# Expert outputs scaled as they are stored and summed into the residual during the last expert, expert biases added at the start, and two norms computed as one chain

## The reference, cut to what matters

```python
def moe(h, ...):                       # h: (512, 1024)
    logits = h @ w_router + b_router   # 32 experts
    top_vals, top_idx = top_k(logits, 4); weights = softmax(top_vals)
    # for every token and each of its four experts e:
    gu = x @ w_gu[e] + b_gu[e]; gate, up = split(gu)
    act = (clip(up, -7, 7) + 1) * min(gate, 7) * sigmoid(1.702 * min(gate, 7))
    y += weight * (act @ w_down[e] + b_down[e])

h = h + g2 * moe(modulate(rmsnorm(h, norm_mlp_w), sh2, sc2), ...)
x = rmsnorm(h, final_norm_w)           # end of the first block
p = rms_norm(x, even_norm) @ even_w_in # start of the second block; x is also its residual
```

## Time and profile before

| | us |
|---|---|
| median of three runs (2360.0 to 2361.71) | 2360.09 |
| the profiled execution, its own time | 2359.39 |
| its span, first to last instruction | 2357.4 |
| TensorE busy | 2215.9 (94%) |
| VectorE busy | 738.2 (31%) |
| mean granted TensorE clock | 0.973 |

### The profile page before, as it was taken

One profiled execution on the slowest core, in us unless ns is written; L12 is line 12 of the kernel. 1 busy time (PEld: TensorE's weight loads), 2 busy tenths in 40 slices (PEclk: granted clock), 3 DMA queues, 4 the chain that ended last, 5 costly groups with the idle time before them and its releaser, 6 DMA issues. The chain is left out here.

```text
span 2357.4 us, 35769 instructions
## 1 busy us (share of the span) xinstructions
PE 2215.9 (94%) x14443; PEld 907.7 (39%) x14443; DVE 738.2 (31%) x1371; ACT 501.8 (21%) x912; POOL 141.1 (6%) x174
## 2 busy tenths in 40 slices
PE   5999877999999999999999972999999998999998
PEld 2434532333333333333333321455445444444443
DVE  1133447222121222222222216003077004356533
ACT  2121222111110111111111102110126002446530
POOL 0000002110011111011111012000000000000000
PEclk9999988999999999999999985999999999999999
DMA  9138529999999999999999943412220121122200
GB/s 362 54 122 312 196 103 356 407 411 416 417 417 415 414 415 417 416 414 417 414 416 414 411 164 120 165 54 101 72 71 1 61 82 39 60 90 90 71 36 36
DMA packets 143111, 556.63 MB, mean 236 GB/s; under 512 B 18485, under 2 KB 34014, under 8 KB 109170
## 3 DMA queue, kind: packets, MB, share of 16 engines
q1 hardware_dynamic: 118662, 512.67, 55.1%
q0 software_dynamic: 10608, 30.31, 3.5%
q10 hardware_dynamic: 13788, 12.93, 1.6%
HBM read 535.78 MB, written 25.03 MB: 238 GB/s over the span
## 5 line engine op out<-in xcount | busy, mean ns | idle before, releaser
L1822 PE MATMUL ps<-ring,xeT 128*32 128x512 f32 x6144 | 669.4, 595 | 6.2 <-ACT xeT L1533 6.2
L1822 PEld LDWEIGHTS ps<-ring,xeT 128*32 128x32 f32 x6144 | 196.3, 110 | 451.1 <-issue 449.0
L1799 PE MATMUL ps<-ring,aT 128*32 128x512 f32 x2048 | 266.4, 592 | 1.0 <-ACT ysb L1637 1.0
L1693 DVE TENSOR_SCALAR gate<-ps 128x768 f32<-128x768 f32 x32 | 30.7, 958 | 551.8 <-PE ps L1822 551.8
L1625 ACT ACTIVATE sig<-gate 128x768 f32<-128x768 f32 x32 | 27.0, 844 | 701.1 <-DVE gate L1693 701.1
L360 PE MATMUL ps<-hT_late,ring 128*128 128x512 f32 x384 | 165.2, 592 | 1.5 <-PEq L2046 1.5
L1807 PE MATMUL ps<-ring,aT 128*32 128x256 f32 x2048 | 157.1, 379 | 0.0
L1807 PEld LDWEIGHTS ps<-ring,aT 128*32 128x32 f32 x2048 | 66.0, 110 | 153.7 <-issue 153.7
L2733 PE MATMUL ps<-hT_late,ring 128*128 128x512 f32 x256 | 110.6, 592 | 1.6 <-PEq L2492 1.6
L360 PE MATMUL ps<-ring,mT 128*128 128x512 f32 x256 | 110.1, 592 | 1.2 <-PEq L2299 1.2
L2746 PE MATMUL ps<-hT_late,ring 128*128 128x512 f32 x256 | 110.5, 592 | 0.0
(11 more groups left out here) (374 smaller groups left out, 2030.7 us busy)
## 6 DMA issues: line engine op xcount, KB each, us to landing
ring<-in_w_gu SPq DMA_DIRECT2D x256, 1024.0 KB, 8.3
ring<-in_w_down SPq DMA_DIRECT2D x128, 1024.0 KB, 7.6
ring<-in_even_w_in SPq DMA_DIRECT2D x18, 1024.0 KB, 6.5
ring<-in_w_ada SPq DMA_DIRECT2D x32, 512.0 KB, 8.3
ring<-in_odd_w_in SPq DMA_DIRECT2D x32, 512.0 KB, 5.2
ring<-in_w_ada SPq DMA_DIRECT2D x8, 1024.0 KB, 23.4
ring<-in_w_in SPq DMA_DIRECT2D x8, 1024.0 KB, 14.5
y_scratch<-ysb ACTq DMA_DIRECT2D x128, 64.0 KB
```

The costliest lines, as they stand in the source:

```text
L1693: nc.vector.tensor_scalar(thirds(gate[:]), part_banks(0), 7.0, None, ALU.min).then_inc(M.gu_read, 1)
L1799: mm = nc.tensor.matmul(quad(Y0, 2 * q + n), acted(k, q), w[:, kk, n * BANK:(n + 1) * BANK], start=first, stop=last)
L1822: mm = nc.tensor.matmul(quad(q, c), left(q), part_columns(w, c), start=start, stop=stop)
```

## The change: what it does

- **Scaling at the store.** ScalarE no longer copies rows from PSUM. VectorE does it in one product with `g2q` (g2 laid out as the rows are) at the end of each step (`read_y`). `g2q` is made by eight copies at the very start of the experts' part.
- **Biases.** b_down times g2, by the turned weights, is four products for each half of the columns: the first half after step 0, the second in the middle of step 1. VectorE adds them to `res` (`add_bias`, four of 128x512 each).
- **Sums during the last expert.** Steps 0, 1 and 31 are written out, steps 2 to 30 are the loop. GpSimd gathers the 16 rows of tiles of experts 0 to 29 as soon as these are stored (weights are zero where the row belongs to a later expert), then four of expert 30, then four of expert 31. VectorE adds each straight to `res` (`sum_rows`), 8 ahead of its work for step 31, 4 behind it, 4 after expert 30's rows are read, and 4 after expert 31's are.
- **The end of the experts.** `down(32)` writes other banks and reads a separate transposed tile (`last_turned`), and there is no product for row numbers ahead of it. The last stores are issued by ScalarE and SyncE, four each.
- **One chain for two norms.** With h = `res` and hw = h * w1b, both sums of squares are taken at once; the second norm's scale is worked out from the two (`pair`). xn = hw * scale is handed to TensorE; the four tiles of `res` are written after that.
- **Places.** hT_late and mT are allocated ahead of the experts and lend their room to the experts' buffers; sgT serves for two buffers of later layers. Seven even-layer weight tiles are loaded in the combining part.

```diff
+                for h in range(2):
+                    for q in range(2):
+                        part = slice((2 * q + h) * QUAD, (2 * q + h + 1) * QUAD)
+                        listing.on(nc.vector.tensor_copy(
+                            g2q[part, 0:2], g2b[part, h * BANK:(h + 1) * BANK].rearrange("p (b n) -> p b n", b=2)))
+                for c in range(4):
+                    part = slice(c * QUAD, (c + 1) * QUAD)
+                    listing.on(nc.vector.tensor_copy(g2q[part, 2], g2b[part, c * 256:(c + 1) * 256]))
                 split_places(list_step, posm[:], place[:], third_of[:])
...
                     nc.vector.transpose(turned[:, 0:W], up[:, 0:W]).then_inc(M.aT_read, 1)
+                    if not first:
+                        read_y(e, Y0)
+
+                def read_y(e, b):
+
+                    dve.wait_ge(M.y_stored, e * 128)
+                    nc.vector.tensor_tensor(thirds(ysb), ps[:, b:b + 2, :].rearrange("p b (h n) -> p (b h) n", h=2)[:, 0:3], g2q,
+                                            ALU.mult).then_inc(M.y_read, 1)
+
+                def add_bias(h):
+
+                    for t in range(NT):
+                        dve.wait_ge(biased.sem, NT * h + t + 1)
+                        cols = slice(h * BANK, (h + 1) * BANK)
+                        bias_added.on(nc.vector.tensor_tensor(res[:, t, cols], res[:, t, cols], bank(Y0 + t), ALU.add))
...
                 weights_and_rows()
+                prepare(0)
+                bdown_loaded.wait(dve)
+                bias_ready.on(nc.vector.tensor_tensor(bdown, bdown, g2b[:], ALU.mult))
+                dve.wait_ge(M.aT_done, 1)
+                bias_ready.on(nc.vector.tensor_copy(wT[:], ps[:, IDS, P:2 * P]))
                 block_step(0, True)
+                add_bias(0)
...
+                prepare(1)
+                add_bias(1)
+                block_step(1, False)
...
+                with dve.Fori(0, E - 3) as i:
+                    prepare(i + 2)
+                    block_step(i + 2, False)
...
+                sum_rows(0, 2 * TOPK)
+                block_step(E - 1, False, last=True)
+                sum_rows(2 * TOPK, 3 * TOPK)
+                dve.wait_ge(M.y_done, 2 * (E - 1))
+                read_y(E - 1, Y0)
+                sum_rows(3 * TOPK, NT * TOPK)
+                dve.wait_ge(M.y_done, 2 * E)
+                read_y(E, Y0 + 2)
+                sum_rows(NT * TOPK, NT * TOPK + NT)
...
+                pool.wait_ge(M.y_stored, 128 * (BEFORE + 1))
+                for n in range(NT * TOPK + NT):
+                    if n >= GB:
+                        pool.wait_ge(row_used.sem, n - GB + 1)
+                    if n == NT * TOPK:
+                        pool.wait_ge(M.y_stored, 128 * (BEFORE + 2))
...
+                pool.wait_ge(M.y_stored, 128 * (E + 1))
+                for t in range(NT):
+                    last_rowed[t].on(nc.gpsimd.indirect_dma_start(
...
-                down(E, 8 + 12 * (E - 1), 0, final=True)
+                block_step(E - 1, 8 + 12 * (E - 2), 0, False, last=True)
+                down(E, 8 + 12 * (E - 1), 0, Y0 + 2, last_turned)
...
+                def join(t):
+                    last_rowed[t].wait(dve)
+                    h_ready.on(nc.vector.scalar_tensor_tensor(out=res[:, t, :], in0=last_rows[:, t, :], scalar=w_end[:, 1, t:t + 1],
+                                                              in1=res[:, t, :], op0=ALU.mult, op1=ALU.add))
+                    h_ready.wait(dve)
+                    h_ready.on(nc.vector.tensor_tensor(hw[:, t, :], res[:, t, :], w1b[:], ALU.mult))
...
+                w1b_loaded.wait(dve)
+                join(0)
+                join(1)
+                means(0)
+                join(2)
+                scale(0)
+                means(1)
+                join(3)
+                scale(1)
+                means(2)
+                scale(2)
+                means(3)
+                scale(3)
                 for t in range(NT):
+                    nc.vector.tensor_scalar(res[:, t, :], hw[:, t, :], pair[:, t, 2:3], None, ALU.mult)
```

More of the change, by code:

```diff
@@ L1619, in _, with block_step @@
                 parted.on(nc.scalar.copy(bparts[third], bgu[third]))
-                def block_step(e, first):
+                def block_step(e, first, last=False):
                     act.wait_ge(M.gu_read, e * 2 + 1)
@@ L1704, in block_step @@
                     dve.wait_ge(M.act_ready, e + 1)
+                    if last:
+                        nc.vector.transpose(last_turned[:, 0:W], up[:, 0:W]).then_inc(M.aT_read, 1)
+                        return
                     if not first:
@@ new lines, in _, with sum_rows @@
+                step(nc.vector.memset(gbuf, 0.0))
+                parted.wait(dve)
+                step(nc.vector.memset(last_rows, 0.0))
+                step(nc.vector.memset(turned[:, W:], 0.0))
+                list_ready.on(nc.vector.memset(rowstat[:, 7, 0:1], 0.0))
+                with dve.Fori(0, E - 3) as i:
+                    prepare(i + 2)
+                    block_step(i + 2, False)
+                def sum_rows(n0, n1):
+                    bias_added.wait(dve)
+                    for n in range(n0, n1):
+                        t = n // TOPK if n < NT * TOPK else n - NT * TOPK
+                        w = w_early[:, n:n + 1] if n < NT * TOPK else w_end[:, 0, t:t + 1]
+                        dve.wait_ge(rowed[n % GB].sem, 16 * (n // GB + 1))
+                        if n:
+                            row_used.wait(dve)
+                        row_used.on(nc.vector.scalar_tensor_tensor(out=res[:, t, :], in0=gbuf[:, n % GB, :], scalar=w,
+                                                                   in1=res[:, t, :], op0=ALU.mult, op1=ALU.add))
@@ L1812, in down, with acted, add_biases @@
                             mm.then_inc(stream.used, 1)
-                def acted(k, q):
+                def acted(k, q, src):
                     at = q * FQ + k * QUAD
-                    return turned[:, at:at + QUAD]
+                    return (turned if src is None else src)[:, at:at + QUAD]
+                def add_biases(h):
+                    for t in range(NT):
+                        rows = slice(t * E, (t + 1) * E)
+                        biased.on(nc.tensor.matmul(bank(Y0 + t), wT[rows, :], bdown[rows, h * BANK:(h + 1) * BANK], start=True,
+                                                   stop=True))
                 def gate_up(left, w, start, stop):
@@ L1823, in gate_up, with block_step @@
                     return mm
-                def block_step(e, m0, turn, first):
+                def block_step(e, m0, turn, first, second=False, last=False):
                     pe.wait_ge(M.xeT_read, e * 8 + 8)
@@ L1838, in block_step @@
                     if not first:
+                        if second:
+                            pe.wait_ge(bias_added.sem, 2 * NT)
                         down(e, m0 + 8, turn)
+                    if last:
+                        return
+                    if first:
+                        pe.wait_ge(bias_ready.sem, 2)
                     pe.wait_ge(M.onehot_ready, e + 4)
@@ L1861, in extra_blocks @@
                     body(i)
+                if after:
+                    after()
         def listed(eng, i):
@@ L2109, in _ @@
+                nc.scalar.activation(rowstat[:, 7, 2:3], ident[:, 0:1], ACT.Sqrt)
                 for t in range(NT):
+                    for i, src in enumerate((res, hw)):
+                        act.wait_ge(h_ready.sem, 2 * t + i + 1)
+                        if t or i:
+                            act.wait_ge(N.sum, 2 * t + i)
+                        nc.scalar.activation(junk1[:], src[:, t, :], ACT.Square, scale=1.0 / 32,
+                                             accum_out=pair[:, t, i:i + 1]).then_inc(N.sum, 1)
```

306 lines of the change are left out of this document (172 added, 134 removed).

## The result

| | before | after |
|---|---|---|
| median | 2360.05 (2359.11 to 2361.71, 4 runs) | 2348.66 (2346.68 to 2349.28, 4 runs) |
| ratio to before, 95% interval | | 0.9944 (0.993 to 0.9958) |
| the profiled execution, its span | 2359.39, 2357.4 | 2349.28, 2347.0 |
| mean granted clock | 0.973 | 0.976 |

The change makes the kernel 11 us faster. 2334 was forecast, with a range up to 2345; the measured time lies outside it. The kernel does what the change says, but more than half of the forecast gain is missing. The trace of after stands some 0.8 us later than before's already at the last routing product, ahead of the experts' part (348.96 against 348.14); a second trace of the same kernel has it at 351.10, so this is a shift from trace to trace.

A forecast was written before the change was run, and what follows sets the result against it. TensorE was taken to bound the experts and VectorE's chain the 75.6 us from the last expert product to the projection. -32.7 + 2.2 + 4.4 = -26.1 us gave 2334.0, own range 2329 to 2339, wider range 2325 to 2345.

The forecast's parts named there:

- Steps of the loop, no cost: Expert loop: `read_y` adds a 0.96 us product 29 times, but VectorE has idle time, so nothing waits.
- The start, +4.4: Start of the experts: g2 copies, bias products and adds make the second `down` 4.4 us later (3.5 to 6.3).
- The end of the experts, no gain on TensorE: Around step 31: eight sums end at 1378.9, TensorE waits 1.4 us, the last product still ends at 1394.2.
- its own signs: Forecast wrong if TensorE waits in the loop or over 5 us before the last `down`, or first join awaits a gather.
- rival B: End of experts: gathers land slowly beside weights (12, then 8 us), last product 7 us later, 2341; chance 0.16.
- From there to the projection, -32.7: Last expert product to even-layer projection: stores, gathers, w1b and norms start the projection at 1437.1, 32.7 us sooner (-29.5 to -35.5).
- GpSimd beside VectorE's sums: Last gathers: the shared-interface rule would slow every gather, costing 3.0 us; the forecast held that only the first was slow.
- The clock, +2.2: Projection: after idle time TensorE starts at half clock, costing 2.2 us (0 to 2.5).
- The sum: Whole kernel: -32.7 + 2.2 + 4.4 = -26.1 us, giving a median of 2334.0.

The follow-up runs named there:

- Light weights: Changed kernel, but only 128 of 1024 columns of w_down loaded for the last two experts, leaving out weights the result needs: 2342.44 us, ratio 0.9925.
- four ahead: Changed kernel with four sums instead of eight ahead of VectorE's work for step 31, the other eight of the twelve behind it: 2347.16 us, ratio 0.9939.
- reads early: Changed kernel with VectorE doing four sums, step 31, then the read of expert 30's rows, and only then sums 5 to 12: 2344.7 us, ratio 0.9932.
- none ahead: Changed kernel with all twelve sums behind VectorE's work for step 31: 2352.91 us, ratio 0.9967.
- three experts at the end: Changed kernel with early gathers taking only experts 0 to 28, expert 29's rows coming as four more gathers and sums: 2335.78 us, ratio 0.9895.

## Why the prediction was wrong, by its own steps

- **Steps of the loop, no cost**: right. TensorE waits nowhere in the loop; the 5.3 to 5.4 us by which the `down` ahead of the last one ends later (1387.8) were there at the second `down`.
- **The start, +4.4**: right in the sum, 4.5 measured, but in part by luck, since errors in its terms cancelled. The copies were dearer (3.7 for 2.6): the first took 1.01 us, the other three of 512 columns 0.42 to 0.50, those of 256 columns 0.29. The forecast had the full clock in step 1, since the first bias products were to fill the idle time ahead of it; 3.54 us of that were left, the granted clock was 0.57 from 396 to 400, and the first 96 products took 11.93 where the next 96 took 10.51. The bias adds (2.44 for 3.0) and products (1.14 for up to 3.4) were cheaper. The forecast let VectorE's row decide; it ended at 418.9, 1.5 ahead of the second `down`, for which TensorE's own row ran without a gap. Eight products of 32 rows by 128 columns took 1.14 us, where eight expert products take 1.04: they ran side by side. What follows starts 1.07 us behind their start, where it is 0.86 with expert products. With what the Trainium skill, "TensorEngine Tiling (Array Packing)", Key Properties, says of such tiles, that they work in parallel, the trace agrees; the drain that it names for a change of the tiling mode can't have been longer than those 0.2 us.
- **The end of the experts, no gain on TensorE**: this is the step that failed. It had expert 29's rows stored 2.5 us behind the last issue and the first gather at 1359, 1364 on after's clock. From the last issue to the gather it took 6.1 us, and the issues 5.4 in place of 3.8, so the gather stood at 1369.57, and with it all sums and step 31's clip behind them. TensorE waited 8.1 us, not 1.4, and lost another 1.8 at half clock: the last product ends 8.8 us later than forecast. By its own signs the forecast was wrong there (over 5 us ahead of the last `down`). Light weights took the wait down to 1.2. It is rival B's place, but not its mechanism: it had the gathers slow to land (12 us; they took 6 to 7), where it was the stores ahead of them. Its case against itself, that the loads end about then, overlooked that they had moved later with everything else: DMA is still full from 1365 to 1370.
- **From there to the projection, -32.7**: 27.7 measured, 5.0 short. From the end of the last read to w1b's issue it took 18.7 us for 11.3. The forecast had four gathers behind the last read; there were eight, since expert 30's stores also landed late (10.7 us from its read to its first gather), and from the end of the last read to the end of the last issue it took 13.7 us for 8.9. The barrier took 4.9 from the last issue to w1b's, not 2.4. The last read itself ended 0.9 later behind the last product than forecast. w1b landed in 3.87 in place of 5.9, and the chain of the norms took 21.3 for 22.5, which gave 3.2 back. As forecast, w1b released the first join. (The heading's bound of -29.5 is -29.7 by the working under it.)
- **GpSimd beside VectorE's sums.** Four of the last eight gathers took 1.40 to 1.85 us in after's first trace, while they took at most 1.12 beside the same sums in its second. The Trainium skill's rule of a shared interface ("GPSIMD Engine Reference", Specifications) would have been 3.0 us; the first trace shows 2.3 and the second none, so sums alone do not decide it.
- **The clock, +2.2**: right, 2.4 (167.6 against 165.2 for the same 384 products).
- **The sum.** On the trace, 8.8 and 5.0 are 13.8 us of projection started late: 2334 + 13.8 = 2347.8, against 2348.66 measured.

But the two terms don't stand side by side, as the single edits show. With TensorE's wait taken away, four ahead and reads early won between -1.4 and 4.4 us of projection, by which of after's traces they are held against, and none ahead lost. The prediction followed TensorE to its last product and then added a tail; the longer path ran past TensorE, from expert 29's stores through five rounds of gathers. That its beginning was on the path is shown by three experts at the end; it should have been worked out as one chain from its first event.

## What to carry to other kernels

When a result must go through HBM and back before the next step, price the store from the traffic it stands beside (here 32 KB landed in 1.9 us alone and in 7.0 beside weight loads), and let nothing wait for the newest one: start from results one step older and treat the newest apart, even if this adds work. When work is moved to run beside the bounding engine, write down the chain of that work from its first event to the end, with the rounds in which its buffers come free; a wait seen on the bounding engine may come from that chain and not be what sets the end. Transfers that a barrier waits for, but whose data nobody needs ahead of it, belong behind it.

## What the runs showed of the hardware

- A store of 32 KB landed in 1.9 us with the DMA engines nearly idle and in a median of 7.0 (up to 8.7) beside weight loads at some 416 GB/s; 64 KB in 1.9 to 6.3.
- The barrier's first instruction came 2.9 to 3.6 us behind GpSimd's last indirect gather in every kernel here; where GpSimd had been idle, 1.6 us behind ScalarE's last issue.
- The same eight GpSimd gathers took 0.99 to 1.12 us or up to 1.85 us each in different executions of one kernel. The cause is open.
- Four idle-time products at the end of a part, 3.7 us in all, saved 2.4 us of half clock in the next.
